# Low halves of 47 more weight panels on GpSimd, and heads, ups and rope tables in another order

## The chip, the cores and the metric

The kernel is one program on one core of a Trainium2 chip. The core has five engines with an instruction queue each: TensorE (PE), which multiplies matrices and loads weights in a second queue beside it (PEld), VectorE (DVE), ScalarE (ACT), GpSimd (POOL) and SyncE (SP), which here only starts the transfers from HBM. The metric is the time of one execution on the device in microseconds (us), as the median of several runs.

## The reference

The input is one sequence of 256 positions by 1024 columns in fp32. It goes through a first block and then through two layers of a second block. All weights are fp32; together they are some 177 MB, and each is used once.

```python
# first block
u = rmsnorm(h, norm_mix); proj = u @ w_in               # 512 + 3 x 512 columns
y_ssm = s5_branch(u_ssm, ...)                           # complex scan over time, gelu, times sigmoid(y @ w_glu)
y_attn = stick_breaking_attention(q, k, v)              # 8 heads of 64
g_ssm, g_attn = split(sigmoid(u @ w_gate + b_gate))
merged = g_ssm * (y_ssm @ w_up_ssm) + g_attn * (y_attn @ w_up_attn)
h = h + merged @ w_out
hid = relu(rmsnorm(h, norm_mlp) @ w_ff1)                # 1024 -> 4096
h = h + (hid * hid) @ w_ff2                             # 4096 -> 1024
# second block, each of two layers
shift, scale, gate = split(silu(c) @ w_ada + b_ada)
u = x * (1 + scale) + shift; proj = u @ w_in            # 7840 columns
a = silu(layer_norm(causal_conv(a1 * sigmoid(a2), 31 taps) + bias)); y_a = (a * silu(a_gate)) @ w_a_out
yb = gb * causal_conv(gc * xb, 3 taps);                 y_b = (yb * silu(b_gate)) @ w_b_out
q, k, v from q_lat @ w_uq and kv_lat @ w_ukv, 32 of 96 columns of q and k turned by rope(cos, sin)
y_c = (softmax_attention(q, k, v) * silu(c_gate)) @ w_c_out       # 8 heads
m = g_a * y_a + g_b * y_b + g_c * y_c                   # g = sigmoid(merge logits)
x = layer_norm(alpha * x + gate * (m @ w_o))
```

`rope_tables` are cos and sin of position times frequency; they are needed from the first layer of the second block on.

## The kernel before

**Tiling.** Activations lie transposed: 128 partitions of channels, 256 positions in the free dimension. A weight arrives as a panel of 128 x 2048 elements, 1 MB: either 8 row tiles of 256 columns, or (the jobs with 512 rows: up_attn, glu, up_ssm, ff2, branch0 to branch2) 4 row tiles of 512 columns. SP walks the list of panels and starts one transfer each into one of four raw buffers.

**Split weights.** A matrix product in full precision is made of three of reduced precision. ACT copies a panel to `w_hi` in the rounded type (L924, `high_halves`); then the low half `w_lo = raw - w_hi` is subtracted by DVE (L1234) or by POOL (L814). The constant `POOL_LOW` (L70) says by job and number which of the two does it, and both walk the same function `low_halves` and leave out the other's. There are three buffers for these halves (HL = 3). The activation has two halves too (`u_hi`, `u_lo`; in the branches `va_hi`, `vb_hi` and so on). PE runs `w_hi` by `x_hi`, `w_hi` by `x_lo` and `w_lo` by `x_hi`, 16 matmuls of 128 x 256 each, all in L1791; 48 of them are one panel. They add up in one of two PSUM banks `pg` (two banks in turn for a panel of 512 columns). A bank is free again when ACT or DVE has taken its content out (`take`, L926 and L1257). The `ada` panels aren't split.

**Order.** `schedule()` (L95) writes one list of steps by hand, ORDER; every engine walks it and does its own part of each step, so that each queue's order follows the list. At the step `panel` PE runs the panel. ACT and DVE (or POOL) first do the halves of the panels up to two further on (`next_splits`, L708), then DVE and ACT take the finished group. So a DVE step that stands after a panel in the list lies behind the low halves of later panels. The transfer into a raw buffer waits until the low half that read it is done (`slot_free`), POOL's or DVE's, and a half waits until PE is done with the panel three before it. On DVE each helper (`tt`, `ts`, `stt`, `copy`, `take`) waits for the instruction before it, on its own semaphore.

**First block, in time.** About 11 us of norm; projections (ssm, q, k, v) to about 70 us; the loop over 8 heads (L181 to L221) to about 190 us; up_attn, glu, up_ssm and the first out panels to about 247 us; the rest of out; the feed-forward to about 470 us. In the loop a head `m` has `stick_weights m-1`, `stick_soft`, two steps `state` of the S5 scan, `stick_fails`, `stick_scores m+1`, `s5_out`, an `ada` and a `gate` panel, and `stick_out m-1`. `bu` is a pair of matmuls (K 32) that feeds a `state`. In `stick_scores` of PE, bu's two parts stand between the two matmuls of the scores:

```python
                pe.matmul(p_z[:, 0:T], k1[rows, f, 0:P], q1[rows, f, :], start=True, stop=True)
                if hd:
                    bu_part(2 * hd - 1, 1).then_inc(*event("bu", 2 * hd - 1))
```

`stick_out` multiplies one head's weights with its values (two matmuls, L1992, L1993). The second block does its attention with `weighted_pair` (L1982), which takes two heads at once.

**Feed-forward.** Eight chunks `c`: two ff1 panels of chunk c, then two ff2 panels of chunk c - 1; all 32 low halves are POOL's already. After chunk 2 stand `rope_tables` (DVE L1595, ACT L1144) and `modulate_columns`. On DVE `rope_tables` zeroes two pads, makes the angles (copy, multiply), calls `turns` (L1432: two scalar steps, three multiply-adds, one clamp), halves the angle, waits for ACT's sines (`rope_sines`) and ends with three steps. ACT's part waits for `rope_angle`.

**Second block, in time, layer 0 (layer 1 is 299 us later).** From about 495 us: latents, conv branch a in parts of multiply-adds on DVE (L1669), uq, ukv, cg; attention with the panels xb, gc, gb, bg, ag between the heads (low halves on POOL already), to about 615 us; then branch1, four merge1, branch2, four merge2, branch0, four merge0 and four w_o panels to about 765 us. A merge panel ends with ACT's sigmoid, a product and a sum on DVE (L1243, `area<-area`). Between them lie the layer norm of branch a (`ln_a_*`, `split a`, ahead of branch0) and `split_tiles`, which makes `m_hi` and `m_lo` for w_o. `normalise` scales the context of a head with the softmax's reciprocals, from SBUF to SBUF; PE transposes the context behind it, and `gate_take` multiplies gates into it.

Of the kernel before, what the change touches and what calls it, by code (L numbers as in the profile page):

```python
# [69 lines left out]
POOL_LOW = [("gate", n) for n in range(3, 8)] + [(job, n) for job in ("ff1", "ff2") for n in range(2 * DFF // W)]  # L70
POOL_LOW += [(job, n) for job in ("xb", "gc", "gb", "bg", "ag") for n in range(2)] + [("merge1", 1), ("merge1", 2)]
# [23 lines left out]
def schedule():  # L95
# [86 lines left out]
    for m in range(HEADS):  # L182
        f = m // 2
        if m:
            step("stick_weights", m - 1)
        step("stick_soft", m)
        if m % 2 and f:
            step("s5_y", f - 1)
        step("state", 2 * m)
        if m + 1 < HEADS:  # L190
            step("gate_ahead", len(panels) + 1)
        step("stick_fails", m)
        step("ada_turn", m)
        if m + 1 < HEADS:
            step("stick_scores", m + 1)
        else:
            step("bu", 2 * m + 1)
        if m:
            step("s5_out", m - 1)
        if m + 1 == HEADS:  # L200
            step("stick_weights", m)
            step("state", 2 * m + 1)
        ada_panel(m + 1)
        step("ada_take", m + 1)
        if 2 * m + 2 < PAIRS:
# [64 lines left out]
    for c in range(chunks + 1):  # L270
        if c < chunks:
            for n in range(2):
                panel("ff1", 0, 2 * c + n, "w_ff1", 0, W * c + 256 * n, KT, 256, 1)
                if c == 0:
# [15 lines left out]
        if c == 2:  # L290
            step("rope_tables")
            step("modulate_columns", 0)
# [151 lines left out]
def build(nc, t, out, marks, dry):  # L444
# [3 lines left out]
    with ctx:  # L448
# [443 lines left out]
        def _(act):  # L892
# [251 lines left out]
            def rope_tables(_, __):  # L1144
# [50 lines left out]
            def ln_affine(l, _):  # L1195
                if l < LAYERS - 1:
                    act.wait_ge(sem("u_rows"), over("u_rows", l + 1, 1))
                for j in range(KT):
# [3 lines left out]
                    elif j < ACT_TILES:  # L1202
# [8 lines left out]
                         rope_tables=rope_tables, prescale=prescale, latent_sums=latent_sums,  # L1211
# [7 lines left out]
        def _(dve):  # L1219
# [375 lines left out]
            def rope_tables(_, __):  # L1595
# [7 lines left out]
                ts(nmean[rows], nmean[rows], freq[rows, 0:1], None, ALU.mult).then_inc(*c.step())  # L1603
                turns(nmean[rows], sin_cos[rows], cos_sin[rows])
                ts(nmean[rows], sin_cos[rows], 0.5, None, ALU.mult).then_inc(*c.event("rope_angle"))
                dve.wait_ge(sem("rope_sines"), over("rope_sines"))
# [134 lines left out]
            def ln_affine(l, _):  # L1741
                if l == LAYERS - 1:
                    before = c.last
                    for j in range(ACT_TILES, KT):
# [7 lines left out]
                         ada_end=ada_end, glu_mul=glu_mul, gate_take=gate_take, modulate=modulate, rope_tables=rope_tables, u2_piece=u2_piece, modulate_columns=modulate_columns,  # L1752
# [8 lines left out]
        def _(pe):  # L1761
# [155 lines left out]
            def bu_ready(r):  # L1917
# [7 lines left out]

            def bu_part(r, comp):
                f, rows = r // FOUR, slice(32 * (r % FOUR), 32 * (r % FOUR) + 32)
                return pe.matmul((p_bu, p_s)[r % 2][:, T * comp:T * comp + T], bt[rows, comp, f, :], ussm[rows, f, :],  # L1928
                                 start=True, stop=True)

            def bu(r, _):
                bu_ready(r)
                bu_part(r, 0)
                bu_part(r, 1).then_inc(*event("bu", r))
# [17 lines left out]
            def stick_scores(hd, _):  # L1952
# [37 lines left out]
            def weighted_values(values, weights, hd):  # L1990
                rows, at = slice(64 * (hd % 2), 64 * (hd % 2) + 64), T * (hd // 2 % 2)
                pe.matmul(p_o[rows, at:at + T], values[:, 0, DH * hd:DH * hd + DH], weights[:, 0:T], start=True, stop=False)  # L1992
                return pe.matmul(p_o[rows, at + P:at + T], values[:, 1, DH * hd:DH * hd + DH], weights[:, T:T + P],  # L1993
                                 start=False, stop=True)
# [148 lines left out]
```

## Time and profile before

| what | value |
|---|---|
| median of 3 runs | 1069.53 us (1066.78 to 1070.15) |
| the profiled execution | 1071.31 us |
| its span | 1069.6 us |
| PE busy | 1020.7 us, 95% of the span |
| PEld busy | 960.3 us, 90% |
| DVE busy | 696.7 us, 65% |
| ACT busy | 545.7 us, 51% |
| POOL busy | 376.4 us, 35% |
| mean granted TensorE clock | 0.981 of full speed |
| moved from and to HBM | 167 GB/s over the span |

A busy time is the sum of an engine's instructions in one profiled execution. Where PE is busy nearly always, another engine's time counts only where PE waits for it. The granted clock is that of TensorE, 1.0 being 2.4 GHz and 0.5 being 1.2 GHz. A wait is put down to the engine that let it go last.

### The profile page before, as it was taken

The page shows a single profiled execution, that of the slowest core. Times are in us where ns is not written, and L with a number is a line of the kernel's source. Part 1 is how long each engine was busy: PE and PEld are TensorE (multiplying, and loading weights), DVE is VectorE, ACT ScalarE, POOL GpSimd, SP SyncE. Part 2 cuts the span into 40 slices and gives each one's busy share as a digit, 9 for nine tenths or more (in the row PEclk, how much of TensorE's full clock was granted, in tenths as well). Part 3 has the DMA queues.
Part 4 walks back from the last instruction along what each step waited for, and adds up shares of the span by engine and source line. Part 5 has one row for each costly group of instructions (what it writes and reads, how often), then busy time and mean ns, then how long its engine had stood idle before and what let it go on. Part 6 is the DMA issues. An engine that isn't in the chain of part 4 may idle for free.

```text
span 1069.6 us, 19601 instructions
## 1 busy us (share of the span) xinstructions
PE 1020.7 (95%) x8132; PEld 960.3 (90%) x8132; DVE 696.7 (65%) x1052; ACT 545.7 (51%) x631; POOL 376.4 (35%) x159
## 2 busy tenths in 40 slices
PE   7998999889999999999999999999999999999996
PEld 6985777779899999989999999999789999999995
DVE  4958788773435322345977986856449789877563
ACT  5455554744544444446654744644366456446442
POOL 3079673003487888710056530000100456300000
PEclk8998999999999999999999999999899999999998
DMA  8642444664774656553744555554556444564601
GB/s 278 197 159 81 157 157 159 222 212 158 242 231 126 194 193 187 186 175 123 237 129 148 161 175 178 160 195 158 153 163 203 153 130 150 182 192 147 209 19 40
DMA packets 159496, 179.58 MB, mean 168 GB/s; under 512 B 5040, under 2 KB 141744, under 8 KB 159408
## 3 DMA queue, kind: packets, MB, share of 16 engines
q1 hardware_dynamic: 159024, 177.22, 52.0%
q8 instruction: 65, 1.06, 0.4%
q0 software_dynamic: 384, 1.10, 0.3%
q14 instruction: 23, 0.19, 0.1%
HBM read 177.26 MB, written 1.05 MB: 167 GB/s over the span
## 4 chain that ended last, share of the span: by engine, by line
PE 76%; DVE 9%; issue 7%; ACT 5%; DMA 2%; POOL 1%; SPq 0%; DVEq 0%; ACTq 0%; POOLq 0%
PE pg L1791 64%; DVE p_bu L1669 2%; ACT w_hi L924 2%; PE p_s L1874 2%; DVE area L1243 2%; PE p_y L1949 1%; ACT u_hi L899 1%; PE pg L1812 1%; PE p_s L1767 1%; DVE area L1261 1%; PE p_s L1928 1%; DVE rows L1285 1%; DVE area L1247 1%; DMA area<-in_c_state 1%; PE p_bu L1928 1%
## 5 line engine op out<-in xcount | busy, mean ns | idle before, releaser
L814 POOL TENSOR_TENSOR w_lo<-raw,w_hi 128x2048 fp32r<-128x2048 f32 x61 | 285.3, 4688 | 316.9 <-ACT w_hi L924 316.9
L924 ACT ACTIVATE w_hi<-raw 128x2048 fp32r<-128x2048 f32 (+3 forms) x153 | 275.1, 1804 | 67.5 <-PE pg L1791 29.3
L1234 DVE TENSOR_TENSOR w_lo<-raw,w_hi 128x2048 fp32r<-128x2048 f32 (+2 forms) x92 | 190.7, 2084 | 61.0 <-ACT w_hi L924 60.8
L1791 PE MATMUL pg<-u_hi,w_hi 128*128 128x256 f32 x1536 | 213.5, 291 | 16.7 <-ACT u_hi L899 11.0
L1791 PEld LDWEIGHTS pg<-u_hi,w_hi 128*128 128x128 f32 x1536 | 195.9, 193 | 27.2 <-issue 11.4
L1791 PE MATMUL pg<-u_lo,w_hi 128*128 128x256 f32 x1536 | 202.9, 285 | 0.0
L1791 PE MATMUL pg<-u_hi,w_lo 128*128 128x256 f32 x1536 | 200.2, 283 | 0.0
L1791 PEld LDWEIGHTS pg<-u_lo,w_hi 128*128 128x128 f32 x1536 | 194.3, 195 | 0.0
L1791 PEld LDWEIGHTS pg<-u_hi,w_lo 128*128 128x128 f32 x1536 | 191.4, 192 | 0.0
L930 ACT ACTIVATE area<-pg 128x512 f32<-128x512 f32 (+1 forms) x92 | 54.1, 588 | 155.5 <-PE pg L1791 143.6
L1669 DVE SCALAR_TENSOR_TENSOR p_bu<-area,par,p_bu 128x256 f32<-128x256 f32 x232 | 93.9, 483 | 0.8
L1261 DVE TENSOR_TENSOR h<-pg,h 128x512 f32<-128x512 f32 x36 | 24.9, 692 | 60.0 <-PE pg L1791 59.0
L1243 DVE TENSOR_TENSOR area<-area 128x512 f32<-128x512 f32 (+5 forms) x67 | 44.2, 660 | 27.0 <-ACT area L930 24.4
L878 POOL TENSOR_SCALAR area<-h,scale,shift 128x256 f32<-128x256 f32 x8 | 8.1, 1019 | 143.1 <-DVE h L1312 143.1
L899 ACT ACTIVATE area<-area 128x512 f32<-128x512 f32 (+7 forms) x53 | 31.7, 598 | 51.7 <-DVE area L1545 47.4
L1791 PE MATMUL pg<-vb_hi,w_hi 128*128 128x256 f32 x320 | 45.8, 285 | 5.1 <-DVE area L1261 3.1
L1791 PE MATMUL pg<-va_hi,w_hi 128*128 128x256 f32 x288 | 41.9, 286 | 5.3 <-ACT w_hi L924 2.4
L1791 PEld LDWEIGHTS pg<-vb_hi,w_hi 128*128 128x128 f32 x320 | 41.3, 191 | 6.3 <-DVE area L1261 3.5
L1791 PE MATMUL pg<-vb_lo,w_hi 128*128 128x256 f32 x320 | 45.2, 283 | 0.0
L1791 PE MATMUL pg<-vb_hi,w_lo 128*128 128x256 f32 x320 | 45.2, 283 | 0.0
L1791 PEld LDWEIGHTS pg<-va_hi,w_hi 128*128 128x128 f32 x288 | 37.5, 192 | 6.6 <-issue 3.0
L1285 DVE RECIPROCAL rows<-root 128x256 f32<-128x256 f32 x11 | 19.3, 1753 | 36.5 <-ACT root L899 36.2
(221 smaller groups left out, 1343.6 us busy)
## 6 DMA issues: line engine op xcount, KB each, us to landing
raw<-in_w_in SPq DMA_DIRECT2D x68, 1024.0 KB, 5.4
raw<-in_w_ff SPq DMA_DIRECT2D x32, 1024.0 KB, 5.6
raw<-in_w_ada SPq DMA_DIRECT2D x24, 1024.0 KB, 5.3
raw<-in_w_gate SPq DMA_DIRECT2D x8, 1024.0 KB, 7.8
raw<-in_w_o SPq DMA_DIRECT2D x8, 1024.0 KB, 5.2
raw<-in_w_out SPq DMA_DIRECT2D x4, 1024.0 KB, 8.7
raw<-in_w_b_out SPq DMA_DIRECT2D x4, 1024.0 KB, 5.1
raw<-in_w_c_out SPq DMA_DIRECT2D x4, 1024.0 KB, 5.5
```

What stands on the lines that cost most here:

```text
L814: pool.tensor_tensor(w_lo[:, s, 0:n], raw[:, r, 0:n], w_hi[:, s, 0:n].bitcast(F32), ALU.subtract).then_inc(sem(f"raw_free{r}"), 1)
L899: return act.activation(out_, in_, func, **kw)
L924: act.activation(dst, src, ACT.Copy).then_inc(*(c.event("w_hi", q["s"]) if i == len(parts) - 1 else c.step()))
L930: act.activation(dst, src, func, **kw).then_inc(*c.bank_free(g))
L1234: ins = dve.tensor_tensor(dst, src, hi.bitcast(F32), ALU.subtract)
L1243: return dve.tensor_tensor(out_, a, b, op)
L1261: dve.tensor_tensor(out_, a, b, op).then_inc(*c.bank_free(g))
L1285: dve.reciprocal(rstd[:, which, :], root[:, which, :]).then_inc(*c.event("rstd", key))
L1669: ins = dve.scalar_tensor_tensor(out=dst, in0=apad[:, j, k:k + T], scalar=w, in1=partial[j], op0=ALU.mult, op1=ALU.add)
L1791: ins = pe.matmul(pg[g % 2][0:m, i * T:i * T + T], w[:, k, a:a + m], x[:, k, :], start=x is x_hi and w is wh and (i, k) == turns[0], stop= ...
L1874: ins = pe.matmul(p_s[:, region * T:region * T + T], ones[:, :], src[:, i, :], start=i == 0, stop=i == KT - 1)
L1928: return pe.matmul((p_bu, p_s)[r % 2][:, T * comp:T * comp + T], bt[rows, comp, f, :], ussm[rows, f, :], start=True, stop=True)
```

## The change

Four things change; what is computed stays the same, and so do the transfers, ACT's high halves and PE's matmuls, except for the paired weighted sums.

1. **POOL_LOW.** These low halves go from DVE to POOL: up_attn, up_ssm and out, panels 0 and 1 of each, and glu 0 (7 panels), and in each of the two layers merge0, merge1, merge2 and w_o, panels 0 to 3 of each, and branch0, branch1 and branch2, both panels (22 panels, of which POOL had merge1 1 and 2 already). That is 7 + 2 x 20 = 47 panels in the list; those that were POOL's before stay with it.
2. **Heads.** `bu` no longer alternates with the scores but runs as a step of its own behind them, in every head. `stick_out` takes two heads at once with `weighted_pair`, at m = 2, 4, 6 and after the loop, and ACT copies the context once for each pair.
3. **Ups.** `high_ahead` (ACT's high halves of the panels ahead) stands before `s5_y`, `s5_gelu` and the table set instead of behind them.
4. **Rope tables.** The step is cut into four, `rope_angles`, `rope_reduced` (the call of `turns`), `rope_half` and `rope_tables` (the last three steps), one behind each ff1 panel of chunks 2 and 3. `modulate_columns` moves from chunk 2 to chunk 4.

```diff
-POOL_LOW = [("gate", n) for n in range(3, 8)] + [(job, n) for job in ("ff1", "ff2") for n in range(2 * DFF // W)]
-POOL_LOW += [(job, n) for job in ("xb", "gc", "gb", "bg", "ag") for n in range(2)] + [("merge1", 1), ("merge1", 2)]
+POOL_LOW = [("gate", n) for n in range(3, 8)] + [(job, n) for job in ("up_attn", "up_ssm", "out") for n in range(2)] + [("glu", 0)] + [(job, n) for job in ("ff1", "ff2") for n in range(2 * DFF // W)]
+POOL_LOW += [(job, n) for job in ("xb", "gc", "gb", "bg", "ag") for n in range(2)]
+POOL_LOW += [(job, n) for job in ("merge0", "merge1", "merge2", "w_o") for n in range(4)]
+POOL_LOW += [(job, n) for job in ("branch0", "branch1", "branch2") for n in range(2)]
...
         if m + 1 < HEADS:
             step("stick_scores", m + 1)
-        else:
-            step("bu", 2 * m + 1)
+        step("bu", 2 * m + 1)
...
+        if m and m % 2 == 0:
+            step("stick_out", m - 2)
...
-        if m:
-            step("stick_out", m - 1)
-    step("stick_out", HEADS - 1)
+    step("stick_out", HEADS - 2)
     step("ada_turn", 10)
     step("s5_out", HEADS - 1)
     step("split", "ctx")
+    step("high_ahead", count["split"] + 2)
     step("s5_y", WT - 1)
     step("s5_gelu")
     step("table_set", "sigmoid_and_others")
-    step("high_ahead", count["split"] + 2)
...
                 panel("ff1", 0, 2 * c + n, "w_ff1", 0, W * c + 256 * n, KT, 256, 1)
+                if c in (2, 3):
+                    step(("rope_angles", "rope_reduced", "rope_half", "rope_tables")[2 * c - 4 + n])
...
-        if c == 2:
-            step("rope_tables")
+        if c == 4:
             step("modulate_columns", 0)
...
             def stick_out(hd, _):      # ScalarE
-                if hd % 2:
-                    i = hd // 2
-                    act.wait_ge(sem("o_stick"), over("o_stick", hd))
-                    fn(context1[:, i, :], p_o[:, T * (i % 2):T * (i % 2) + T], ACT.Copy).then_inc(*c.event("ctx", i))
+                i = hd // 2
+                act.wait_ge(sem("o_stick"), over("o_stick", i))
+                fn(context1[:, i, :], p_o[:, T * (i % 2):T * (i % 2) + T], ACT.Copy).then_inc(*c.event("ctx", i))
...
             def stick_weights(hd, _):      # VectorE
-                    dve.wait_ge(sem("o_stick"), over("o_stick", hd - 2))
+                    dve.wait_ge(sem("o_stick"), over("o_stick", (hd - 2) // 2))
...
             def stick_scores(hd, _):      # TensorE
-                if hd:
-                    bu_ready(2 * hd - 1)
-                    bu_part(2 * hd - 1, 0)
                 pe.matmul(p_z[:, 0:T], k1[rows, f, 0:P], q1[rows, f, :], start=True, stop=True)
-                if hd:
-                    bu_part(2 * hd - 1, 1).then_inc(*event("bu", 2 * hd - 1))
...
             def stick_out(hd, _):      # TensorE
-                pe.wait_ge(sem("w_stick"), over("w_stick", hd))
+                pe.wait_ge(sem("w_stick"), over("w_stick", hd + 1))
-                if hd >= 2:
+                if hd:
                     pe.wait_ge(sem("ctx"), over("ctx", hd // 2 - 1))
-                weighted_values(v1, stick_w[:, hd % 2], hd).then_inc(*event("o_stick", hd))
+                weighted_pair(v1, stick_w, hd).then_inc(*event("o_stick", hd // 2))
```

## Rows read from the trace of the kernel before

**Rows 1.** Windows: busy us of PE, PEld, DVE, ACT, POOL; clock; DMA share; GB/s.
```profile
191.00:247.00 56.00, 47.82 (x410) 42.51 (x406) 41.05 (x39) 28.58 (x30) 0.00 (x0) 0.97 0.64 207
...
622.00:740.00 118.00, 116.22 (x951) 115.39 (x952) 86.26 (x101) 58.84 (x57) 10.23 (x2) 1.00 0.53 170
...
208.00:212.00 4.00, 4.00 (x26) 4.00 (x25) 3.90 (x4) 2.18 (x2) 0.00 (x0) 0.66 0.64 233
```

**Rows 2.** Groups by line and shape, whole span: busy us, mean ns of one.
```profile
L814 POOL TENSOR_TENSOR w_lo<-raw,w_hi 128x2048 fp32r<-128x2048 f32 x61 | 285.3, 4688 | 316.9 <-ACT w_hi L924 316.9
...
L1234 DVE TENSOR_TENSOR w_lo<-raw,w_hi 128x2048 fp32r<-128x2048 f32 x78 | 178.7, 2294 | 59.9 <-ACT w_hi L924 59.7
```

**Rows 3.** Timeline: start, duration (us), instruction, [idle before, releaser]. POOL beside DVE.
```profile
345.31 5.07 POOL L814 TENSOR_TENSOR w_lo<-raw,w_hi 128x2048 fp32r<-128x2048 f32 x1
...
633.99 4.63 POOL L814 TENSOR_TENSOR w_lo<-raw,w_hi 128x2048 fp32r<-128x2048 f32 x1 [0.16 <-ACT w_hi L924]
...
637.96 1.21 DVE L1243 TENSOR_TENSOR area<-area 128x512 f32<-128x512 f32 x1 [2.22 <-ACT area L930]
```

**Rows 4.** Chain of waits in order of time, heads: start, us, what.
```profile
71.80 0.63 PE p_z L1963 x2
...
72.42 0.23 PE p_z L1966 x2
...
126.72 0.58 PE p_o L1992 x2
...
127.30 0.22 PE p_o L1993 x2
...
128.93 0.62 PE p_s L1928 x2
...
130.81 0.41 PE p_z L1966 x2
...
187.45 1.06 PE p_s L1928 x4
```

**Rows 5.** Timeline: a paired weighted sum and what PE does next.
```profile
603.29 0.65 PE L1982 MATMUL p_o<-area 128*64 128x256 f32 x4
...
604.09 0.55 PE L2032 MATMUL p_c<-ident,area 128*128 128x128 f32 x3
```

**Rows 6.** Timeline of 195 to 242 us.
```profile
197.25 1.22 DVE L1243 TENSOR_TENSOR va_lo<-area,va_hi 128x1024 fp32r<-128x1024 f32 x1
...
206.45 1.35 PE L1791 MATMUL pg<-va_hi,w_hi 128*128 128x256 f32 x8 [2.44 <-ACT w_hi L924]
...
241.53 0.74 PE L1791 MATMUL pg<-u_hi,w_hi 128*128 128x256 f32 x4 [0.78 <-ACT u_hi L899]
```

**Rows 7.** Timeline of the feed-forward stage.
```profile
323.09 1.26 DVE L1243 TENSOR_TENSOR vb_lo<-area,vb_hi 128x512 fp32r<-128x512 f32 x1 [1.42 <-ACT vb_hi L899]
...
324.93 4.64 POOL L814 TENSOR_TENSOR w_lo<-raw,w_hi 128x2048 fp32r<-128x2048 f32 x1 [1.14 <-ACT w_hi L924]
...
326.78 1.92 ACT L924 ACTIVATE w_hi<-raw 128x2048 fp32r<-128x2048 f32 x1 [1.93 <-issue]
...
335.38 1.33 DVE L1251 SCALAR_TENSOR_TENSOR rows<-rows 64x256 f32<-64x256 f32 x3
...
351.83 0.35 PE L1791 MATMUL pg<-vb_hi,w_hi 128*128 128x256 f32 x1 [1.95 <-issue]
```

**Rows 8.** Timeline at the end of attention, layer 0.
```profile
604.32 4.64 POOL L814 TENSOR_TENSOR w_lo<-raw,w_hi 128x2048 fp32r<-128x2048 f32 x1 [2.25 <-ACT w_hi L924]
...
606.71 1.91 ACT L924 ACTIVATE w_hi<-raw 128x2048 fp32r<-128x2048 f32 x1
...
608.24 1.20 DVE L1247 TENSOR_SCALAR area<-area,rsum 128x128 f32<-128x128 f32 x2
```

**Rows 9.** Timeline of the merge stage, layer 0.
```profile
673.30 1.76 DVE L1247 TENSOR_SCALAR area<-area,par 128x256 f32<-128x256 f32 x4
...
729.98 0.74 PE L1791 MATMUL pg<-m_hi,w_hi 128*128 128x256 f32 x4 [0.67 <-ACT m_hi L899]
```

More of the change, by code:

```diff
@@ L1138, in stick_out, with rope_half @@
             def stick_out(hd, _):
-                if hd % 2:
-                    i = hd // 2
-                    act.wait_ge(sem("o_stick"), over("o_stick", hd))
-                    fn(context1[:, i, :], p_o[:, T * (i % 2):T * (i % 2) + T], ACT.Copy).then_inc(*c.event("ctx", i))
-            def rope_tables(_, __):
+                i = hd // 2
+                act.wait_ge(sem("o_stick"), over("o_stick", i))
+                fn(context1[:, i, :], p_o[:, T * (i % 2):T * (i % 2) + T], ACT.Copy).then_inc(*c.event("ctx", i))
+            def rope_half(_, __):
                 act.wait_ge(sem("rope_angle"), over("rope_angle"))
@@ L1210, in _ @@
                          stick_scores=stick_scores, stick_weights=stick_weights, stick_out=stick_out,
-                         rope_tables=rope_tables, prescale=prescale, latent_sums=latent_sums,
+                         rope_half=rope_half, prescale=prescale, latent_sums=latent_sums,
                          latent_roots=latent_roots, scores=scores, turn=turn, ln_a_squares=ln_a_squares, ln_a_var=ln_a_var,
@@ L1593, in gate_take, with rope_angles @@
                     take(g, bconv[:, 2 * n:2 * n + 2, :], both, bconv[:, 2 * n:2 * n + 2, :], ALU.mult)
-            def rope_tables(_, __):
+            def rope_angles(_, __):
                 for pad in (apad[:, :, 0:CONV_A - 1], bpad[:, :, 0:CONV_B - 1]):
@@ L1603, in rope_tables, with rope_reduced, rope_half @@
                 ts(nmean[rows], nmean[rows], freq[rows, 0:1], None, ALU.mult).then_inc(*c.step())
+            def rope_reduced(_, __):
+                rows = slice(NOPE, P)
                 turns(nmean[rows], sin_cos[rows], cos_sin[rows])
+            def rope_half(_, __):
+                rows = slice(NOPE, P)
                 ts(nmean[rows], sin_cos[rows], 0.5, None, ALU.mult).then_inc(*c.event("rope_angle"))
+            def rope_tables(_, __):
+                rows = slice(NOPE, P)
                 dve.wait_ge(sem("rope_sines"), over("rope_sines"))
@@ L1751, in _ @@
                          stick_scores=stick_scores, stick_soft=stick_soft, stick_weights=stick_weights,
-                         ada_end=ada_end, glu_mul=glu_mul, gate_take=gate_take, modulate=modulate, rope_tables=rope_tables, u2_piece=u2_piece, modulate_columns=modulate_columns,
+                         ada_end=ada_end, glu_mul=glu_mul, gate_take=gate_take, modulate=modulate, rope_angles=rope_angles, rope_reduced=rope_reduced, rope_half=rope_half, rope_tables=rope_tables, u2_piece=u2_piece, modulate_columns=modulate_columns,
                          latent_norm=latent_norm, rope_k=rope_k, rope_q=rope_q, conv_a=conv_a, conv_b=conv_b, scores=scores,
@@ L1915, in s5_turn, with bu @@
                 ins.then_inc(*event("bt_ps"))
-            def bu_ready(r):
+            def bu(r, _):
                 pe.wait_ge(sem("bt"), over("bt", 1))
@@ L1924, in bu_ready @@
                     pe.wait_ge(sem("root"), over("root", ("norm", 0)))
-            def bu_part(r, comp):
                 f, rows = r // FOUR, slice(32 * (r % FOUR), 32 * (r % FOUR) + 32)
[L1928 to L1934, printed above, removed]
+                bank_ = (p_bu, p_s)[r % 2]
+                for comp in range(2):
+                    ins = pe.matmul(bank_[:, T * comp:T * comp + T], bt[rows, comp, f, :], ussm[rows, f, :],
+                                    start=True, stop=True)
+                ins.then_inc(*event("bu", r))
             def s5_out(j, _):
@@ L1988, in weighted_pair @@
                 return ins
[L1990 to L1994, printed above, removed]
             def stick_out(hd, _):
-                pe.wait_ge(sem("w_stick"), over("w_stick", hd))
+                pe.wait_ge(sem("w_stick"), over("w_stick", hd + 1))
                 for s, v in emptied(groups_of("v")):
                     pe.wait_ge(s, v)
-                if hd >= 2:
+                if hd:
                     pe.wait_ge(sem("ctx"), over("ctx", hd // 2 - 1))
-                weighted_values(v1, stick_w[:, hd % 2], hd).then_inc(*event("o_stick", hd))
+                weighted_pair(v1, stick_w, hd).then_inc(*event("o_stick", hd // 2))
             def latent_stats(l, _):
```

## The prediction

> **What bounds the kernel now.** I read the page first, then the busy time by stage, the chain of waits in order of time, and the timeline at every place where TensorE (PE) stands still. PE is busy for 1020.7 of 1069.6 us, so only what lies on PE's path moves the time. The stages differ. The merge stages have next to nothing to win: in 118 us PE works 116.2 and VectorE (DVE) 86.3. From 191 to 247 us (up_attn, glu, up_ssm, first out panels) PE is idle for 8.2 of 56 us [rows 1]. GpSimd (POOL) is 35% busy, which makes it look like free room. It is not quite free: its low half of a panel takes 4.69 us on average where DVE's takes 2.29 [rows 2].
>
> The row that matters most is another one. At 637.96 DVE starts a multiplication with both inputs in SBUF, which takes 0.69 us elsewhere. It takes 1.21, and ends 0.55 us after POOL's low half ends (633.99 + 4.63) [rows 3]. Every such instruction that I found beside a low half of POOL looks like this, as do the scalings from SBUF to SBUF; instructions with one input in PSUM do not. When POOL has its next low half ready, DVE's one waiting instruction goes first and POOL takes 5.07 instead of 4.62 us [rows 3], and the DVE instruction behind it then waits for a whole low half again. The Trainium skill ("SBUF — State Buffer", practical consequences) says the same of a DVE instruction with two SBUF inputs and of a GpSimd one that reads SBUF: the two exclude each other for a whole instruction. By this rule the time comes out as forecast below, without it as in rival A; the trace agrees for single instructions.
>
> **The change, part by part.** All is summed against the profiled execution, 1071.3 us (span 1069.6 and 1.7 around it); that lies 1.8 us above the median of the three runs, 1069.5.
>
> *Heads, on PE's path.* Before, a head's bu matmuls and scores alternate: from 128.93 to 131.22 (130.81 + 0.41) is 2.29 us. Not alternated, the scores take 0.63 + 0.23 and bu 1.06 [rows 4], together 1.92. That saves 0.37 for each of six heads, 2.2 us. The first head is bound by DVE and the last is not alternated already. A single weighted sum takes 0.58 + 0.22 = 0.80 us [rows 4]; a pair, as the second block has it, runs from 603.29 to 604.09, also 0.80 [rows 5]. Six singles in the bound stretch become three pairs, 2.4 us; the last pair lies in a wait. Nothing waits for the pair: the copy behind it on ACT is 0.4 us and the weights are ready some 3 us earlier. Heads: **-4.6**, between -3.5 and -5.5.
>
> *191 to 247 us.* Seven low halves leave DVE. This takes away the 2.44 us before up_attn 1 [rows 6], where bank takes were queued behind a low half. But POOL's low half of up_attn 0 starts at 195.1 as DVE's did, and ends at 199.7. The subtraction va_lo (1.22 us, at 197.25 before [rows 6]) now ends at 200.8; s5_y behind it moves too; s5_gelu's two-input step meets the next low half and ends at 206.5 instead of 201.4, the takes at 207.2, so up_attn 1 starts 0.8 us later in spite of all. vb_lo meets glu's low half (ends 215.3, was 211.8) and the takes behind it free the bank for glu 0 at 216.0: 2.4 us late. In up_ssm the adds into `merged` (both inputs SBUF) meet the low halves of up_ssm 1, out 0 and out 1, one each; u_hi's last piece comes at 247.1, and the last quarter of out 0's first pass, at 241.53 before [rows 6], starts 5.6 us late. **+5.6**. If scalar_tensor_tensor with two SBUF inputs isn't held (no row shows one clearly held) it is +3.7; if all is hidden, -6.4.
>
> *Rope tables.* Before they ran after a feed-forward pair, with ACT waiting in them and so POOL starved; the price was the 1.95 us before 351.83 [rows 7]. After, rope_reduced sits between the subtraction of ff1 5 (323.09 + 1.26 = 324.35) and the takes of ff2. POOL asks at 324.93. Two of its six steps fit ahead; the third waits until 329.6, the fourth for a second low half (its w_hi is ready at 328.7 [rows 7]) until 334.5. The last steps (0.42 us each for the multiply-adds, as 1.33 for three [rows 7]) end at 335.5, and the take at 336.3. PE's third ff2 group needs that bank at 326.5: a stall of 9.8 us. Less the 1.95: **+7.9**. If multiply-adds aren't held, one low half is left: +2.1. rope_tables' own three steps end 0.5 us too late for the next low half, a matter of phase: 0 taken, up to +4. The angles, rope_half and modulate_columns fit into POOL's pauses: 0.
>
> *End of attention, both layers.* DVE's two scalings of the last head are at 608.24 and 609.08 (1.20 us for both), POOL's low half ends at 608.96, and branch1 0's w_hi is ready at 608.6 [rows 8]. Before, its low half was DVE's at 610.95. Now POOL takes it at once, and the second scaling waits for its end at 613.7. The transposes on PE (610.4) and the gate takes behind the scaling follow at 613.9 and 615.4 instead of 611.1: +4.3 a layer, **+8.6**. The gain of two low halves off DVE (4.6 us) is worth nothing there, because the convolution steps that end last wait for a matmul at 618. At least 0, if the second scaling slips in.
>
> *Branches, merges, w_o, both layers.* From 20 of 22 panels DVE's 2.29 us go; PE wasn't waiting for them. POOL now has 4.62 us of each panel's 5.76, and merges 0 and 2 need two two-input steps a panel: 4.62 + 2 x 0.69 = 6.0 us. Through the three-deep slots POOL may lag some 8 us. DVE may not: in merge2 it has eight merge steps, four scalings and five wide steps of the a branch. The scalings at 673.30 [rows 9] wait until 677.8, one merge step until 684.4, one until 691.0, ln_a_out ends at 693.6, and vb_hi is ready at 694.7, vb_lo at 696.3, where PE wants them at 692.4 and 695.7: 3.0 us. In merge0 every panel's two steps are separated by a low half; the last m_hi comes about 4.3 us after the 729.98 [rows 9] that it has now (shift taken out). Per layer +7.3, **+14.6**; from +1 (only the wait of the first step, slots absorb the rest) to +24.
>
> *Clock.* In 208:212 the granted clock was 0.66 [rows 1], after the 2.44 us gap: 3.4 us at 1.2 GHz, half of it lost, 1.7 us. The gap of 1.95 brought none. Of some nine new stalls of 2.4 to 10 us I count four at 1.5: **+6.0**, 0 to +14.
>
> **Sum:** 1071.3 - 4.6 + 5.6 + 7.9 + 8.6 + 14.6 + 6.0 = 1109.4 in the profile's terms; less 1.8, **1107.6, rounded 1107 us**, 3.5% slower.
>
> **Rivals.**
> *A, DVE's relief wins (faster).* The point is in the gaps between DVE's dependent steps: if POOL doesn't get in there, each chain waits at most once and the waits stay behind PE. Then go 4.6 (heads), the four gaps of 191 to 247 us behind DVE's low halves (2.4, 1.5, 1.6 and 0.8, the first in [rows 6]), 1.95, and a clock fall (1.5): 1069.5 - 14.5 = 1055. Against it: POOL's request lies open at the end of its last low half, and the 5.07 us row gives it the turn right behind one DVE step. For it: no row shows two dependent steps of DVE around an open low half of this length. It decides where the stalls together stay under 4.6 to 14 us.
> *B, held, but absorbed.* Multiply-adds aren't held and the slots carry the merges: -4.6 + 3.7 + 2.1 + 8.6 + 2 + 1.5 = +13.3, 1083. For it: the three slots, and ACT's order starves POOL as soon as DVE is late, which frees DVE. Against it: the low halves of the last merge panel lie just where m_hi is wanted.
> *C, saturated.* rope_tables is caught (+4), the merges cost 20 and the clock 10: 1069.5 + 51.5 = 1121.
>
> **Chances.** Forecast 0.52, B 0.21, A 0.21, C 0.06. A alone is more than the 2 in 10 that may be left out, so the range goes down to its time and half of it is in: 1055 to 1122; left out are A's lower half and the outer half of C with the clock's upper end. The forecast's own range, with its terms' bounds of clock and merges, is 1090 to 1122. What this kernel's measurement can tell from no change is about 0.3% (3 us). Faster by more 0.20 (A, less the part of it whose gains cancel), within 0.04 (that part, and the low end of B), slower 0.76.
>
> **What would show it.** In the changed kernel: va_lo at about 197 takes 3 to 4 us; PE idle near 205, 214 and 240 to 247; a PE gap of about 10 us in the feed-forward at 321 (= 326 - 4.6), with DVE's `rows<-rows` steps of 4 to 5 us; the second scaling of the last head 4.5 us long with PE idle before its transposes; `area<-area` steps with a mean well above 0.8 us in the merges and PE idle before branch0 and w_o; clock falls at these places. Wrong if these steps keep their lengths of before, or if they are long and PE stays gapless. The heads should each take some 0.7 us less in any case.

## The result, and the profile after

The changed kernel takes **1122.57 us** (median of 4 runs, 1120.03 to 1122.89) against 1069.05 us for the kernel before (4 runs). The ratio is 1.0498, with a 95% interval of 1.0475 to 1.0522: 5.0% slower. The forecast was 1107 us, slower, with a range up to 1122; the direction is right, the time lies 0.6 us outside the range.

The page of the changed kernel, the lines that answer to the table of before. The parts are: span; busy time by engine; busy tenths in 40 slices and PE's granted clock; the chain that ended last by engine and by line; three groups of instructions (busy us, mean ns of one).

```profile
span 1121.1 us, 19594 instructions
PE 1030.7 (92%) x8132; PEld 977.2 (87%) x8132; DVE 700.7 (62%) x1005; ACT 545.6 (49%) x631; POOL 599.7 (53%) x206
...
POOL 3088873533974478710066667684100556676950
PEclk8999999989989799989999899999899999999988
...
PE 59%; DVE 25%; issue 8%; ACT 5%; DMA 1%; POOL 1%; DVEq 0%; SPq 0%; ACTq 0%; POOLq 0%
PE pg L1801 54%; DVE area L1244 9%; DVE area L1248 3%; DVE p_bu L1679 2%; PE p_s L1884 2%; ACT w_hi L926 1%; ACT u_hi L901 1%; DVE p_bu L1244 1%; DVE rows L1286 1%; DVE area L1252 1%; DVE p_bu L1464 1%; DVE p_s L1244 1%; DVE m_lo L1244 1%; DVE area L1262 1%; DVE p_s L1464 1%
...
L816 POOL TENSOR_TENSOR w_lo<-raw,w_hi 128x2048 fp32r<-128x2048 f32 x108 | 508.6, 4717 | 349.4 <-ACT w_hi L926 349.1
...
L1244 DVE TENSOR_TENSOR area<-area 128x512 f32<-128x512 f32 (+5 forms) x67 | 98.2, 1466 | 62.5 <-ACT area L932 60.0
L1235 DVE TENSOR_TENSOR w_lo<-raw,w_hi 128x2048 fp32r<-128x2048 f32 (+5 forms) x45 | 83.1, 1870 | 24.1 <-ACT w_hi L926 24.0
```

On the page of the kernel before, the same chain and the same two DVE groups read:

```profile
PE 76%; DVE 9%; issue 7%; ACT 5%; DMA 2%; POOL 1%; SPq 0%; DVEq 0%; ACTq 0%; POOLq 0%
...
L1234 DVE TENSOR_TENSOR w_lo<-raw,w_hi 128x2048 fp32r<-128x2048 f32 (+2 forms) x92 | 190.7, 2084 | 61.0 <-ACT w_hi L924 60.8
...
L1243 DVE TENSOR_TENSOR area<-area 128x512 f32<-128x512 f32 (+5 forms) x67 | 44.2, 660 | 27.0 <-ACT area L930 24.4
```

Three things are to be read here. DVE gave 47 low halves away (92 are 45 now), and yet its busy time went from 696.7 to 700.7 us: what it was freed of (190.7 - 83.1 = 107.6 us) came back as longer steps. The step `area<-area` alone, 67 times as before, went from 44.2 us (mean 660 ns) to 98.2 us (1466 ns). On the chain that ended last DVE has 25% where it had 9%. And POOL, busy for 53% of the span, has 1% of that chain: it isn't late, it is in the way.

The span grew by 51.5 us. PE's idle time grew from 48.9 us (1069.6 - 1020.7) to 90.4 us (1121.1 - 1030.7), by 41.5 us. PE's busy time grew by 10.0 us with almost the same work; that is the clock (18.2 us, worked out below), less what the heads and small differences save. Set side by side, the start of the same piece of PE's work in the two traces:

| piece of work on PE | before | after | later by |
|---|---|---|---|
| gate 3, first matmul | 120.71 | 115.77 | -4.9 |
| up_attn 0 | 198.00 | 187.50 | -10.5 |
| out 1 | 247.37 | 246.04 | -1.3 |
| ff2 3, behind the rope steps | 326.53 | 334.51 | +8.0 |
| ff1 8 | 357.66 | 379.05 | +21.4 |
| branch1 0, `vb_lo` | 618.95 | 647.46 | +28.5 |
| w_o 0, last quarter of the first pass [rows 9] | 729.98 | 765.19 | +35.2 |
| end of the span | 1069.6 | 1121.1 | +51.5 |

**The rope steps**, timeline of the changed kernel (start and duration in us, in brackets the idle time before and what ended it). They answer to [rows 7].

```profile
322.82 0.62 DVE L1248 TENSOR_SCALAR rows<-rows 64x256 f32<-64x256 f32 x2
...
323.37 9.18 POOL L816 TENSOR_TENSOR w_lo<-raw,w_hi 128x2048 fp32r<-128x2048 f32 x2 [1.14 <-ACT w_hi L926]
323.47 9.82 DVE L1252 SCALAR_TENSOR_TENSOR rows<-rows 64x256 f32<-64x256 f32 x3
...
334.51 2.05 PE L1801 MATMUL pg<-va_hi,w_hi 128*128 128x256 f32 x8 [9.39 <-issue]
...
355.06 14.18 POOL L816 TENSOR_TENSOR w_lo<-raw,w_hi 128x2048 fp32r<-128x2048 f32 x3 [5.88 <-ACT w_hi L926]
...
356.49 3.76 DVE L1244 TENSOR_TENSOR va_lo<-area,va_hi 128x512 fp32r<-128x512 f32 x1 [1.75 <-ACT va_hi L901]
...
360.35 4.54 DVE L1252 SCALAR_TENSOR_TENSOR rows<-rows 64x256 f32<-64x256 f32 x1
364.92 4.79 DVE L1248 TENSOR_SCALAR rows<-rows 32x256 f32<-32x256 f32 x2
...
370.61 0.77 PE L1801 MATMUL pg<-vb_hi,w_hi 128*128 128x256 f32 x2 [10.84 <-issue]
```

The three multiply-adds took 1.33 us in [rows 7]; now they take 9.82, and end 0.7 us after POOL's two low halves (323.37 + 9.18 = 332.55). PE stands still for 9.39 us until DVE has taken its bank. The same happens once more at 360 us: three low halves of POOL without a pause, and three steps of DVE behind one another (`va_lo`, a multiply-add, a scalar step), each waiting for one of them.

**The end of attention**, layer 0, the same view, against [rows 8]:

```profile
626.22 9.13 POOL L816 TENSOR_TENSOR w_lo<-raw,w_hi 128x2048 fp32r<-128x2048 f32 x2 [2.26 <-ACT w_hi L926]
...
629.94 0.17 DVE L1709 RECIPROCAL rsum<-sums 128x2 f32<-128x2 f32 x1
...
630.14 5.36 DVE L1248 TENSOR_SCALAR area<-area,rsum 128x128 f32<-128x128 f32 x2
...
635.55 0.55 PE L2026 MATMUL p_c<-ident,area 128*128 128x128 f32 x3 [3.28 <-DVE area L1248]
...
637.24 0.55 PE L1801 MATMUL pg<-u_hi,w_hi 128*128 128x256 f32 x1 [1.14 <-DVE area L1262]
```

The two scalings took 1.20 us and take 5.36; the reciprocal just ahead of them also reads only SBUF, beside the same low half of POOL, and keeps its 0.17 us. So not every form of instruction is held.

**Merges and the out panels**, one of PE's long waits behind such a step in each:

```profile
232.85 4.10 DVE L1244 TENSOR_TENSOR area<-area 128x512 f32<-128x512 f32 x1
236.99 0.63 ACT L901 ACTIVATE u_hi<-area 128x512 fp32r<-128x512 f32 x1 [4.30 <-DVE area L1244]
...
237.67 1.22 PE L1801 MATMUL pg<-u_hi,w_hi 128*128 128x256 f32 x4 [4.09 <-ACT u_hi L901]
...
757.70 4.66 POOL L816 TENSOR_TENSOR w_lo<-raw,w_hi 128x2048 fp32r<-128x2048 f32 x1 [1.07 <-ACT w_hi L926]
...
758.01 4.90 DVE L1244 TENSOR_TENSOR m_lo<-area,m_hi 128x512 fp32r<-128x512 f32 x1
...
765.19 0.83 PE L1801 MATMUL pg<-m_hi,w_hi 128*128 128x256 f32 x4 [2.83 <-ACT m_hi L901]
```

PE's wait is put down to ACT here, but ACT itself waited for DVE (4.30 us), and DVE for POOL's low half.

### The profile page after: what moved, and what is told of

Same layout as the page of the kernel before. It is cut to its first block, busy times and chain, and to the rows that moved or that the text cites. A ratio compares the mean times of both kernels' runs of the same rounds, so it can differ in the third digit from the quotient of the medians.

```text
span 1121.1 us, 19594 instructions
## 1 busy us (share of the span) xinstructions
PE 1030.7 (92%) x8132; PEld 977.2 (87%) x8132; DVE 700.7 (62%) x1005; ACT 545.6 (49%) x631; POOL 599.7 (53%) x206
## 4 chain that ended last, share of the span: by engine, by line
PE 59%; DVE 25%; issue 8%; ACT 5%; DMA 1%; POOL 1%; DVEq 0%; SPq 0%; ACTq 0%; POOLq 0%
PE pg L1801 54%; DVE area L1244 9%; DVE area L1248 3%; DVE p_bu L1679 2%; PE p_s L1884 2%; ACT w_hi L926 1%; ACT u_hi L901 1%; DVE p_bu L1244 1%; DVE rows L1286 1%; DVE area L1252 1%; DVE p_bu L1464 1%; DVE p_s L1244 1%; DVE m_lo L1244 1%; DVE area L1262 1%; DVE p_s L1464 1%
## 5 line engine op out<-in xcount | busy, mean ns | idle before, releaser
L816 POOL TENSOR_TENSOR w_lo<-raw,w_hi 128x2048 fp32r<-128x2048 f32 x108 | 508.6, 4717 | 349.4 <-ACT w_hi L926 349.1
L1801 PE MATMUL pg<-u_hi,w_hi 128*128 128x256 f32 x1536 | 219.7, 296 | 21.8 <-ACT u_hi L901 13.2
L1801 PEld LDWEIGHTS pg<-u_hi,w_hi 128*128 128x128 f32 x1536 | 201.7, 199 | 32.7 <-ACT u_hi L901 11.2
L1801 PE MATMUL pg<-u_lo,w_hi 128*128 128x256 f32 x1536 | 206.1, 288 | 0.0
L1801 PEld LDWEIGHTS pg<-u_lo,w_hi 128*128 128x128 f32 x1536 | 197.5, 198 | 0.0
L1244 DVE TENSOR_TENSOR area<-area 128x512 f32<-128x512 f32 (+5 forms) x67 | 98.2, 1466 | 62.5 <-ACT area L932 60.0
L1235 DVE TENSOR_TENSOR w_lo<-raw,w_hi 128x2048 fp32r<-128x2048 f32 (+5 forms) x45 | 83.1, 1870 | 24.1 <-ACT w_hi L926 24.0
L1801 PE MATMUL pg<-vb_hi,w_hi 128*128 128x256 f32 x320 | 48.1, 294 | 21.0 <-issue 13.5
L1801 PE MATMUL pg<-va_hi,w_hi 128*128 128x256 f32 x288 | 42.6, 289 | 12.2 <-issue 9.4
L1801 PEld LDWEIGHTS pg<-va_hi,w_hi 128*128 128x128 f32 x288 | 38.1, 195 | 13.4 <-issue 12.4
L1801 PE MATMUL pg<-vb_lo,w_hi 128*128 128x256 f32 x320 | 48.6, 297 | 0.4 <-DVE vb_lo L1244 0.4
L1801 PEld LDWEIGHTS pg<-vb_lo,w_hi 128*128 128x128 f32 x320 | 44.5, 205 | 0.7 <-DVE vb_lo L1244 0.6
```

Of the source, the lines that this page charges most:

```text
L816: pool.tensor_tensor(w_lo[:, s, 0:n], raw[:, r, 0:n], w_hi[:, s, 0:n].bitcast(F32), ALU.subtract).then_inc(sem(f"raw_free{r}"), 1)
L1235: ins = dve.tensor_tensor(dst, src, hi.bitcast(F32), ALU.subtract)
L1244: return dve.tensor_tensor(out_, a, b, op)
L1801: ins = pe.matmul(pg[g % 2][0:m, i * T:i * T + T], w[:, k, a:a + m], x[:, k, :], start=x is x_hi and w is wh and (i, k) == turns[0], stop= ...
```

## The experiments

Theory H (held): a DVE instruction with two inputs in SBUF, or an elementwise scalar step from SBUF to SBUF, waits until POOL's running instruction is done. Its rivals are named with each run.

**The order alone, and the lists alone.** The two halves of the change, each by itself. The first keeps the POOL_LOW of before in the changed kernel, the second sets the new POOL_LOW into the kernel before:

```diff
-POOL_LOW = ... + [(job, n) for job in ("up_attn", "up_ssm", "out") for n in range(2)] + [("glu", 0)] + ...
-POOL_LOW += [(job, n) for job in ("merge0", "merge1", "merge2", "w_o") for n in range(4)]
-POOL_LOW += [(job, n) for job in ("branch0", "branch1", "branch2") for n in range(2)]
+POOL_LOW = ... + [("merge1", 1), ("merge1", 2)]
```

> The changed kernel with the POOL_LOW of before: only the order of heads, ups and rope tables is changed, the 47 new low halves stay on DVE. Theory H (a DVE instruction that reads two inputs in SBUF waits for the whole low half that POOL is working on): the two stalls of PE at the rope steps (9.39 and 10.84 us in the changed kernel) stay, since the feed-forward's low halves were POOL's before too; with the clock they cost 23 us there. The heads give 11.5 us, as in the changed kernel. 1069 + 23 - 11.5 = 1080 us, all of the stalls from 620 us on gone. Rival L (the 47 new low halves cost the time themselves, because POOL takes 4.7 us for one where DVE takes 2.3): everything but the heads goes away, 1058 us.

> The kernel before with the POOL_LOW of the change and nothing else. Theory H: up_attn to out costs some 9 us, each layer some 15 us (6.6 at the end of attention, 8.3 in the merges and w_o), the rope step stays at its 1.95 us, the heads don't change: 1069 + 39 = 1108 us. Rival L: the lists hold the whole loss and the order only gains, 1069 + 53.5 + 11.5 = 1134 us.

Measured: the order alone 1082.07 us, ratio 1.0129 (1.0094 to 1.0163); the lists alone 1108.74 us, ratio 1.0365 (1.0342 to 1.0388). Theory H had 1080 and 1108, rival L 1058 and 1134. The two parts nearly add up: +12.6 and +39.2 us, together 51.8, against +53.5 in the whole. The order alone costs time although it moves no work at all, because the feed-forward's low halves were POOL's before. Its rope stalls are those of the changed kernel to 0.01 us (9.39 and 10.85): the same three multiply-adds take 9.83 us.

```profile
312.51 9.83 DVE L1250 SCALAR_TENSOR_TENSOR rows<-rows 64x256 f32<-64x256 f32 x3
322.37 0.29 DVE L1246 TENSOR_SCALAR rows<-rows 64x256 f32<-64x256 f32 x1
```

**Low halves in four pieces.** If DVE waits for an instruction of POOL, a shorter instruction makes a shorter wait.

```diff
-                    pool.tensor_tensor(w_lo[:, s, 0:n], raw[:, r, 0:n], w_hi[:, s, 0:n].bitcast(F32),
-                                       ALU.subtract).then_inc(sem(f"raw_free{r}"), 1)
+                    for at in range(0, n, n // 4):
+                        to = at + n // 4
+                        ins = pool.tensor_tensor(w_lo[:, s, at:to], raw[:, r, at:to], w_hi[:, s, at:to].bitcast(F32),
+                                                 ALU.subtract)
+                    ins.then_inc(sem(f"raw_free{r}"), 1)
```

> The changed kernel with each of POOL's low halves cut into four instructions of 128x512. Theory H: what a DVE instruction waits for is one instruction of POOL, now some 1.2 us; DVE gets its turn behind each piece. The stalls of PE shrink to a quarter or vanish (rope 9.4 + 10.8 to some 4 + 4), area<-area falls from 1.47 to below 1.0 us on average: 1075 us, between 1062 and 1092. Theory L, or contention that slows both engines in proportion to what they move: POOL's work is as long as before or longer, the time stays at 1120 us or above.

Measured: 1086.70 us, ratio 1.0154 (1.0106 to 1.0202), inside H's range and 12 us above its value. The lists, the order and the elements that POOL subtracts are the same, and POOL is even busy for longer (575.7 us for 508.6), yet 36 of the 53 us are gone. The rope steps, first in the timeline of DVE and POOL, then POOL's group over the whole span (busy us, mean ns of one):

```profile
318.80 3.39 DVE L1255 SCALAR_TENSOR_TENSOR rows<-rows 64x256 f32<-64x256 f32 x3
...
319.22 5.37 POOL L818 TENSOR_TENSOR w_lo<-raw,w_hi 128x512 fp32r<-128x512 f32 x4 [1.66 <-ACT w_hi L929]
...
322.22 1.24 DVE L1251 TENSOR_SCALAR rows<-rows 64x256 f32<-64x256 f32 x1
...
L818 POOL TENSOR_TENSOR w_lo<-raw,w_hi 128x512 fp32r<-128x512 f32 x432 | 575.7, 1369 | 251.4 <-ACT w_hi L929 251.3
```

A scalar step of 0.29 us that is held takes 1.24 us here; in the changed kernel such a step, where it was held (at 364.92), took 4.47. The first rope stall is 4.44 us instead of 9.39, the second 3.29 instead of 10.84. One expectation failed. `area<-area` should have fallen below 1.0 us and is at 1.36 us on average. There are more waits now, each shorter, and POOL pays too: a low half in pieces takes 5.5 us (4 x 1.369) where it took 4.7. Two of the 67 steps took 9.05 us each, through seven pieces of POOL in a row (the first of them in the second row, whose other step takes 0.69 us):

```profile
714.65 10.07 POOL L818 TENSOR_TENSOR w_lo<-raw,w_hi 128x512 fp32r<-128x512 f32 x8
...
716.22 9.78 DVE L1247 TENSOR_TENSOR area<-area 128x512 f32<-128x512 f32 x2 [13.96 <-ACT area L935]
```

So DVE gets its turn behind one instruction of POOL nearly always, but not always. Why not here, and at the same place of the second layer, stays open.

**The rope steps back in one block.** In the changed kernel, all four rope steps and `modulate_columns` behind chunk 2, as before:

```diff
-                if c in (2, 3):
-                    step(("rope_angles", "rope_reduced", "rope_half", "rope_tables")[2 * c - 4 + n])
...
-        if c == 4:
+        if c == 2:
+            for kind in ("rope_angles", "rope_reduced", "rope_half", "rope_tables"):
+                step(kind)
             step("modulate_columns", 0)
```

> The changed kernel with the four rope steps and modulate_columns back in one block behind chunk 2 of the feed-forward, as before; POOL_LOW as changed. Theory H, with the rope steps held between PE's bank takes: 23 us less and the old 1.95 us back, 1122.5 - 21 = 1101 us. Rival R (the stalls at 325 and 360 us come from the transfers or from ACT's high halves, which the rope steps only happen to lie beside): under 5 us less, 1118 us or more.

Measured: 1098.64 us, ratio 1.0277 (1.0252 to 1.0302): 23.9 us less than the changed kernel, where H had 21. In the stretch from 325 to 370 us of that kernel PE is idle for 1.9 us; in the changed kernel it is idle for 20.2 of 46 us. The two windows (columns as in [rows 1]), first with the block, then as changed:

```profile
325.00:370.00 45.00, 43.06 (x346) 42.79 (x345) 19.98 (x33) 20.27 (x18) 33.02 (x7) 0.96 0.57 173
```

```profile
325.00:371.00 46.00, 25.77 (x196) 25.50 (x195) 27.78 (x18) 14.52 (x13) 26.35 (x6) 0.80 0.42 131
```

**Is it the place of the steps or POOL beside them?** The order as changed, the POOL_LOW of before, less ten low halves around the rope steps:

```diff
+POOL_LOW = [at for at in POOL_LOW if at not in [("ff1", n) for n in range(5, 10)] + [("ff2", n) for n in range(2, 7)]]
```

> The kernel with the changed order and the POOL_LOW of before (1082 us), but the ten low halves around the rope steps (ff1 5 to 9, ff2 2 to 6) are DVE's. Theory H: no low half of POOL lies beside the four rope steps any more, each multiply-add takes 0.42 us, and both stalls (9.39 and 10.85 us) vanish: 1082 - 21 = 1061 us; DVE's own ten low halves of 2.29 us fit. Rival R (the place of the rope steps between PE's bank takes is the cause, whoever subtracts): the stalls shrink by less than half, 1072 us or more.

Measured: 1066.44 us, ratio 0.9956 (0.9939 to 0.9974). That is 15.6 us less than 1082 and not 21, about midway between the two theories (1061 and 1072). The three multiply-adds take 1.33 us again, so the holding is gone. But the queue of DVE isn't free of cost at this place either: its own low half stands between the rope step and the bank take, which is at 317.23 where it could have been at some 315.

```profile
313.33 1.33 DVE L1251 SCALAR_TENSOR_TENSOR rows<-rows 64x256 f32<-64x256 f32 x3
...
315.02 2.29 DVE L1234 TENSOR_TENSOR w_lo<-raw,w_hi 128x2048 fp32r<-128x2048 f32 x1
...
317.23 1.48 DVE L1261 TENSOR_TENSOR h<-pg,h 128x512 f32<-128x512 f32 x2
...
318.01 1.19 PE L1800 MATMUL pg<-va_hi,w_hi 128*128 128x256 f32 x8 [2.91 <-ACT w_hi L925]
```

PE's waits are 2.91 us here and 1.08 + 3.12 us at 340 to 347 us, 7.1 us for the 20.2 of before. By these waits some two thirds of the rope's loss are the holding, and the other third is the place together with DVE's own low halves at it. By the times it is nearer three quarters: heads and ups alone, with the rope steps in their block, take 1061.18 us (below), the order alone 20.9 us more, and this kernel 5.3 more.

**One low half.** In the changed kernel only branch1 0 goes back to DVE:

```diff
-POOL_LOW += [(job, n) for job in ("branch0", "branch1", "branch2") for n in range(2)]
+POOL_LOW += [(job, n) for job in ("branch0", "branch1", "branch2") for n in range(2) if (job, n) != ("branch1", 0)]
```

> The changed kernel, only the low half of branch1 0 in both layers back on DVE. Theory H: the 4.5 us scaling of the last head (it waits for just this low half) takes 0.35 us again, PE's gaps of 3.3 and 1.1 us before the context's transposes and behind them vanish, with the clock fall behind them: 6.6 us a layer, 1122.5 - 13 = 1109 us. Rival (another low half or DVE's own 2.3 us takes the place at once): under 4 us in both layers together, 1119 us or more.

Measured: 1110.18 us, ratio 1.0371 (1.0347 to 1.0396), 12.4 us less for one low half in each layer. The two scalings take 1.18 us again, the gate take (636.43) follows 0.9 us behind them, and PE's waits of 3.28 and 1.14 us are one of 0.45, as before the change (0.46):

```profile
634.34 1.18 DVE L1248 TENSOR_SCALAR area<-area,rsum 128x128 f32<-128x128 f32 x2
...
636.33 0.49 PE L2026 MATMUL p_c<-ident,area 128*128 128x128 f32 x3
636.43 0.69 DVE L1262 TENSOR_TENSOR area<-pg,area 128x512 f32<-128x512 f32 x1
...
637.04 2.28 DVE L1235 TENSOR_TENSOR w_lo<-raw,w_hi 128x2048 fp32r<-128x2048 f32 x1
...
637.27 1.43 PE L1801 MATMUL pg<-u_hi,w_hi 128*128 128x256 f32 x10 [0.45 <-DVE area L1262]
```

DVE's own low half (2.28 us, at 637.04) stands behind the take in its queue. There the order of the queue protects the scalings and the take; nothing in the program keeps a low half of POOL out of the scalings' way. The falls of the clock that the changed kernel has at 636 and 950 us are absent from this trace too.

**What the clock adds.** PE gets work whose result nobody reads while it stands still in the two rope stalls of the order alone:

```diff
+                if (c, n) in ((2, 1), (3, 1)):
+                    step("keep_clock", 40 if c == 2 else 46)
                 panel("ff2", 0, 2 * (c - 1) + n, "w_ff2", W * (c - 1), 512 * n, WT, 512, 2)
```

> The kernel with the changed order and the POOL_LOW of before (1082 us), and in the two rope stalls PE runs matmuls whose result nobody reads: 40 pairs of 0.223 us before ff2 3 (8.9 of the 9.4 us) and 46 before ff2 5 (10.3 of the 10.8). Theory C (the falls of the granted clock to 0.5 at 317 and 351 us come from PE's stillness, and cost half of the 4.1 and 5.7 us that PE worked in them): both falls vanish, 1082 - 5 = 1077 us. Rival (the falls come with the work itself or by chance): the falls stay somewhere in the stretch, 1082 us or more.

Measured: 1076.33 us against 1082.07, ratios 1.0052 (1.0034 to 1.0071) and 1.0129 (1.0094 to 1.0163). The held chains are as long as without the filling (9.87 us for the three multiply-adds), so the gain is put down to the clock. In the two falls PE had worked 4.1 and 5.7 us at half clock, which costs 4.9 us. That the rest of the 5.7 us is clock too isn't shown: in these two traces the falls elsewhere differ as well (two of the order alone, at 481 and 782 us, are absent with the filling). The same stretch without and with the filling, 1.4 us later in the second (the third figure from the end is the granted clock, 0.83 and 1.00):

```profile
304.00:360.00 56.00, 35.76 (x279) 35.41 (x279) 33.54 (x27) 20.08 (x19) 32.60 (x7) 0.83 0.44 134
```

```profile
305.40:361.40 56.00, 54.88 (x468) 54.56 (x467) 33.81 (x27) 20.11 (x19) 32.69 (x7) 1.00 0.46 143
```

**The edits without a loss.** The kernel before with heads and ups alone; then the same with matmuls that nobody reads in two more idle places:

```diff
-    step("keep_clock", 10)
+    step("keep_clock", 24)
...
+                if (c, n) == (3, 1):
+                    step("keep_clock", 8)
                 panel("ff2", 0, 2 * (c - 1) + n, "w_ff2", W * (c - 1), 512 * n, WT, 512, 2)
```

> The kernel before with two of the four edits alone: heads (bu apart from the scores, paired weighted sums) and high_ahead ahead of s5_y; POOL_LOW and the rope step stay as before. Theory H has no loss left in it: the heads took 5.7 to 6.3 us off between the third gate panel and up_attn in four traces, and with the low halves on DVE the moved high_ahead took another 3 us off at up_attn. 1069 - 9 = 1060 us, 1057 to 1063. Rival (the gain of the heads in those traces is only a fall of the clock that happened to be elsewhere): 1066 to 1069 us.

> The kernel with heads and ups changed alone (1061 us), with matmuls whose result nobody reads in two places where PE stands still: 14 pairs of 0.223 us more at the start (3.1 of the 3.9 us before the first panel) and 8 (1.8 of 1.95 us) at the rope step. Theory C: the falls of the clock at 16.5 and 340.8 us, in which PE worked 4.7 and 3.4 us at half clock, vanish: 4 us less, 1057 us. Rival: they move to another place, or the second gap at 17.9 us (1.7 us) brings the first one all the same: 1060 us or more.

Measured: heads and ups alone 1061.18 us, ratio 0.9906 (0.9884 to 0.9928), the 9 us expected. With the filling 1058.09 us, ratio 0.9901 (0.9869 to 0.9933); the two ratios to the kernel before can't be told apart, so the second is no shown gain. In its profile the fall at the rope step is gone (clock 1.00 from 330 to 350 us), but the first fall has only moved from 16.5 to 18.7 us: the rival was right there. Heads and ups alone beat both kernels.

## Why the prediction was right or wrong

**The mechanism was right.** The places that were named came: va_lo takes 3.57 us at 186.66, the first rope stall is 9.39 us (forecast 9.8), the last scaling takes 4.52 us, PE's gaps behind it sum to 4.0 us more than before (forecast 4.3), and the run with branch1 0 on DVE shows that it hangs on this one low half. In the stage of up_attn to out, PE's idle time went from 8.2 of 57 us to 14.4 of 64: +6.2, forecast +5.6. The two windows, before and after:

```profile
190.00:247.00 57.00, 48.82 (x428) 43.13 (x424) 42.02 (x40) 29.57 (x31) 0.00 (x0) 0.97 0.63 204
```

```profile
182.00:246.00 64.00, 49.64 (x395) 44.32 (x394) 42.96 (x30) 27.46 (x27) 34.87 (x7) 0.89 0.55 180
```

Rival A needed steps that slip in between POOL's low halves; the row of 9.82 us for three multiply-adds rules it out. Rival B's condition, that multiply-adds aren't held, fell with the same row.

**Rival C named the time, but not by its terms.** C had 1121 us, 1.6 us from the measured time, with a chance of 0.06. Its direction was right in that the last rope steps are caught and the clock costs more. But it put +4 on those steps, 10 us on the clock and 20 on the merges, where the traces show 10.8, 18.2 and some 9. That these misses cancel is luck.

**Heads: somewhat more than forecast.** Forecast -4.6, between -3.5 and -5.5. From gate 3 to up_attn 0, five of the eight heads, PE needs 5.6 us less (77.3 to 71.7), of which 1.7 are a clock fall at 145.9 us that the changed order doesn't have: -3.9. Over the whole loop, from the first scores (71.73 and 72.41) to up_attn 0, it is 11.2 us less; another fall, at 94.7 us, was 10.2 us long in the profile of before and 3.4 in that of the change, which is 3.4 us of cost, so some 6.1 us are left. The other traces of the changed order have that second fall at 3.4 or at 10.2 us, so that this part is chance. Alone, heads and ups gave 9 us.

**Ups.** With the low halves on DVE the earlier high halves are worth some 3 us up to glu 0: in the order alone up_attn 0 starts 9.3 us earlier than before, up_attn 1 11.4 and glu 0 12.5. The prediction gave them no term of their own; with the low halves on POOL nothing of it is left, since up_attn 1 waits for a bank that a held step blocks.

**The step that failed first: rope_tables.** "rope_tables' own three steps end 0.5 us too late for the next low half, a matter of phase: 0 taken, up to +4". It is 10.84 us of standing still, so that the rope steps cost 9.39 + 10.84 - 1.95 = 18.3 us of PE's time where 7.9 were forecast. The working took POOL's next low half from the trace of before. In the changed kernel the first stall had moved PE's work, va_lo was held as well (3.76 us), and each of the next two steps then asked just behind the start of another low half. A held step ends just behind the start of POOL's next low half, and the step behind it then waits for that one; once a chain is caught, it costs a low half for each step for as long as POOL has the next one ready. What looked like a matter of phase sustains itself.

**The step that failed most: the clock.** Forecast +6.0, from four falls of which each costs 1.5 us. Worked out from the granted clock and PE's busy time, PE worked 67.7 us at half clock after and 31.3 before, which costs 18.2 us more (half of the difference); without the falls that went in the heads (5.1 us) it is some 23 us. There were nine new falls, not four, and the time that PE worked in them comes to 41.3 us, 2.3 us of cost for each. Those at the long stalls were longer than the 3.4 us of the one that the price was taken from: 10.2 us at the 9.39 us stall, 13.7 at the 10.84 us one, both beginning while PE stood still, with 4.5 and 6.0 us of its work in them.

**Merges and w_o: right in kind, too high in size.** Forecast +7.3 a layer; PE's waits there grew by 4.8 us in layer 0 (2.6 before branch0 for 3.0, and 3.4 at the last quarter of the first w_o pass for 1.2 before, where 4.3 more had been forecast). This cancelled part of the misses above.

The sum in PE's idle time: forecast 5.6 + 7.9 + 8.6 + 14.6 = 36.7, measured 41.5. The sum of the forecast was 38.1 us above the profile of before, the span grew by 51.5: of the 13.4 us between them the clock has 12.2 (18.2 for 6.0), PE's idle time 4.8, and the heads and small differences of PE's busy time take some 3.6 back. The range's upper end, 1122, was set below its own terms: the upper bounds of clock (+14) and merges (+24) alone give 1107.6 + 8.0 + 9.4 = 1125 us, and with the +4 of rope_tables 1129. The time is just above the range; that it isn't further off is owed to the merges, which came out some 5 us below their term in both layers together.

## What to carry to other kernels

Ahead of moving work to GpSimd, list the elementwise VectorE steps between TensorE's banks and its next operand that read and write SBUF only, and charge each of them a whole GpSimd instruction, one after another; an engine at 35% may still be in the way. Where such a chain must run beside GpSimd, cut GpSimd's instructions short or keep the one low half that it meets on VectorE (two low halves were worth 12.4 us here). And where TensorE must stand still, count the slow clock behind the stall, or fill it.

## What the runs showed of the hardware

- A multiply-add with both inputs in SBUF is held like a subtraction (4.73 us for a 64x256 step that takes 0.42 us), and so are small scalar steps from SBUF to SBUF (4.5 us for a 32x256 step). For multiply-adds the trace of before had left it open.
- Not everything that reads only SBUF is held. Of the steps that begin at least 0.2 us ahead of the end of a low half of POOL in the changed kernel's trace, all 23 sums `area<-area` of 128x512 are longer than their 0.69 us, while all 12 reciprocals `rsum<-sums` keep their 0.17 us and all 24 reductions `p_y<-area`, which write PSUM, their 0.30 and 0.43. Steps with an input in PSUM keep theirs, as `area<-pg,area` does (0.69 us, 13 of 13).
- The holding goes by the instruction of GpSimd, not by its work: with pieces of a quarter a scalar step takes 1.24 us instead of 4.47, at the price of 0.8 us more for each low half of POOL.
- Seven pieces in a row could still keep VectorE out for 9.05 us, in 2 of 67 steps; this is unexplained.
- With TensorE kept busy through two stalls of 9.4 and 10.9 us the granted clock stayed at 1.00 (2.4 GHz), where it had fallen to 0.5 (1.2 GHz) for 10.2 and 13.7 us (0.83 on average in the stretch). By the medians 5.7 us are gained.
